# Gates of tokens 32 to 127 for the upper 64 expert blocks: from one-hot matmuls to indirect transfers

## The reference, cut to what matters

```
q = (xc @ wq).reshape(PEER_CHUNK, PEER_HEADS, 2, PEER_QDIM // 2)
sc = einsum('thpd,pkd->thpk', q, subkeys)
sv, si = top_k(sc, 16)
cv, ci = top_k((sv[:, :, 0, :, None] + sv[:, :, 1, None, :]) flattened, 16)
i1, i2 = the two key numbers of each chosen pair
e = i1 * 128 + i2                       # one of 16384 experts
g = softmax(cv)
act = gelu(einsum('td,thkd->thk', xc, u[e]))
out = einsum('thk,thkd->td', g * act, v[e])
```

## Time and profile before

| what | value |
|---|---|
| median of 3 runs | 1022.46 us (1022.28 to 1023.46) |
| the profiled execution | 1022.54 us, of it 1020.7 us span from the first to the last instruction |
| PE busy | 1011.5 us, 99% of the span |
| DVE, ACT, POOL busy | 834.3, 649.5, 459.3 us |
| granted clock of TensorE | 1.00 in every slice |
| first half of U, second half of U, V | about 270 to 457, 457 to 654, 654 to 1017 us |

### The profile page before, as it was taken

How to read it: one execution, slowest core, us unless ns; L and a number is a source line. 1 busy time by engine, 2 the same in 40 slices (tenths; PEclk the granted TensorE clock), 3 DMA queues, 4 the chain that set the end, 5 groups by cost and what they waited for, 6 DMA issues and landing times.

```text
span 1020.7 us, 20443 instructions
## 1 busy us (share of the span) xinstructions
PE 1011.5 (99%) x6302; PEld 894.7 (88%) x6302; DVE 834.3 (82%) x1611; ACT 649.5 (64%) x1192; POOL 459.3 (45%) x308
## 2 busy tenths in 40 slices
PE   8999999999999999999999999999999999999998
PEld 6798989999999999998888888888888888888887
DVE  6768786788899999988788888898888887777775
ACT  6456777666555444567877887877777764554543
POOL 0010321008148858867777770134344345545453
PEclk9999999999999999999999999999999999999999
DMA  8664565556467776666677775566665666666663
GB/s 328 264 216 151 187 198 179 187 168 223 146 166 191 190 190 167 184 180 176 173 177 165 174 176 170 162 223 192 205 197 196 206 232 225 211 219 221 211 224 115
DMA packets 89473, 198.20 MB, mean 194 GB/s; under 512 B 26320, under 2 KB 42832, under 8 KB 89424
## 3 DMA queue, kind: packets, MB, share of 16 engines
q1 hardware_dynamic: 68544, 188.99, 56.2%
q0 software_dynamic: 20736, 8.46, 7.3%
q10 hardware_dynamic: 144, 0.14, 0.1%
HBM read 187.01 MB, written 10.55 MB: 194 GB/s over the span
## 4 chain that ended last, share of the span: by engine, by line
PE 95%; DVE 3%; ACT 1%; DMA 1%; issue 0%; SPq 0%; POOL 0%; ACTq 0%; DVEq 0%
PE bank L900 34%; PE bank L875 12%; PE bank L876 6%; PE bank L831 5%; PE bank L833 5%; PE bank L832 5%; PE bank L385 2%; PE bank L844 2%; PE bank L386 2%; PE bank L387 2%; PE bank L451 2%; PE bank L771 2%; PE bank L455 1%; PE bank L467 1%; PE bank L468 1%; PE bank L469 1%
## 5 line engine op out<-in xcount | busy, mean ns | idle before, releaser
L1211 ACT ACTIVATE hi<-raw 128x1024 fp32r<-128x1024 f32 x253 | 269.0, 1063 | 260.7 <-PE bank L900 130.2
L1720 DVE TENSOR_TENSOR lo<-raw,hi 128x1024 fp32r<-128x1024 f32 x253 | 310.9, 1234 | 96.0 <-ACT hi L1211 92.3
L2036 POOL DMA_INDIRECT gate_d<-chosen_w,chosen_at x128 | 250.0, 1953 | 104.4 <-issue 50.5
L2053 POOL TENSOR_TENSOR auxl<-big,auxh 128x256 fp32r<-128x256 f32 x127 | 160.7, 1265 | 196.5 <-ACT auxh L1238 196.4
L875 PE MATMUL bank<-x,hi 128*128 128x512 f32 x512 | 183.9, 401 | 0.0
L900 PE MATMUL bank<-hi,auxh 128*128 128x512 f32 x504 | 157.2, 393 | 1.4 <-POOL auxl L2060 1.4
L900 PE MATMUL bank<-hi,auxl 128*128 128x512 f32 x504 | 155.7, 390 | 0.0
L900 PE MATMUL bank<-lo,auxh 128*128 128x512 f32 x504 | 155.5, 390 | 0.0
L831 PE MATMUL bank<-x,hi 128*128 128x256 f32 x512 | 145.3, 284 | 1.5 <-DVE lo L1720 1.5
L832 PE MATMUL bank<-x,hi 128*128 128x256 f32 x512 | 144.9, 283 | 0.0
L833 PE MATMUL bank<-x,lo 128*128 128x256 f32 x512 | 144.9, 283 | 0.0
(11 more groups left out here) (395 smaller groups left out, 1802.2 us busy)
## 6 DMA issues: line engine op xcount, KB each, us to landing
raw<-u_d SPq DMA_DIRECT2D x128, 512.0 KB
raw<-v_d SPq DMA_DIRECT2D x128, 512.0 KB
raw<-wpre_d SPq DMA_DIRECT2D x70, 512.0 KB
gate_d<-big POOLq DMA_DIRECT2D x16, 512.0 KB, 5.3
gring<-gate_d SPq DMA_DIRECT2D x128, 64.0 KB, 3.0
big<-wpre_d SPq DMA_DIRECT2D x8, 512.0 KB, 9.1
gate_d<-chosen_w,chosen_at POOLq DMA_INDIRECT x128
big<-x_d SPq DMA_DIRECT2D x4, 256.0 KB, 3.9
```

Source lines behind the costliest of these rows:

```text
L1211: act.activation(hi[:, slot(n), :], raw[:, splits(n) % RING, :], ACT.Copy).then_inc(hi_done, 1)
L1720: dve.tensor_tensor(lo[:, slot(n), :], raw[:, splits(n) % RING, :], hi[:, slot(n), :].bitcast(F32), ALU.subtract).then_inc(lo_done, 1)
L2036: pool.indirect_dma_start(gate_d, bass.IndirectOffsetOnAxis(chosen_at[:, d:d + 1], 0), chosen_w[:, P + d:P + d + 1], None, compute_op=ALU. ...
L2053: pool.tensor_tensor(auxl[:, s * T:(s + 1) * T], big[:, bass.ds(i * (UNROLL * T) + b * T, T)], auxh[:, s * T:(s + 1) * T].bitcast(F32), AL ...
```

## The change: what it does

1. Blocks 64 to 127, tokens 64 to 127: a second table `mid_d`. Each choice of a token has one of two cells, by whether its number is under 64 or not, so that one indirect transfer carries two choices of each of 64 tokens. 64 transfers.
2. Blocks 64 to 127, tokens 32 to 63: a third table `few_d`, with four cells, and four choices of each of 32 tokens in a transfer. 32 transfers.
3. The one-hot groups of blocks 64 to 127 are left for tokens 0 to 31: 8 groups in place of 32, one every eighth tile of V. V's first half is written out in place of a loop of 12 steps.
4. POOL issues these 96 transfers after its 128 old ones, and ahead of them 10 small transfers that move addresses and weights between partitions. SP waits for all of them before it loads tile 64 of V and what comes behind it. Both new tables are cleared by 8 transfers each (the upper half of each table), in the attention stage.
5. POOL no longer splits the gated blocks of V's first half: `w_lo` for blocks 0 to 63 is on DVE now. POOL takes it up again from block 64.
6. In V's second half SP fetches three pieces for a block, and DVE adds the two cells (`mid_sum`), sums the four (`few_sum`), and multiplies 224 columns in place of 128 (`gate_block_mid`).
7. DVE makes the addresses of the new transfers (8 small operations) at the end of U's first half.

```diff
+MID = P // 2
+FEW = P // 4
+NGRP_V = FEW // 4
...
-        gring = sb("gring", [P, GRING, P])
+        gring = sb("gring", [P, GRING, 3 * P])
...
             each_tile(sp, HALF - GRING, v_and_gates)
...
-            each_tile(sp, HALF, lambda i, j: v_and_gates(i, HALF - GRING + j))
+            sp.wait_ge(mid_scattered, 16 * MID)
+            sp.wait_ge(few_scattered, 16 * FEW)
+            each_tile(sp, HALF, lambda i, j: v_and_gates(i, HALF - GRING + j, mid=True))
...
             def g_and_v(i, j):
-                if j % 2 == 0:
-                    g_group(i, NGRP + 1 + j // 2, GT)
+                if j % 8 == 0 and j < 8 * (NGRP_V - 1):
+                    g_group(i, NGRP + 1 + j // 8, GT)
                 v_tile(i, j, 1)
...
+            def mid_sum(i, m):
+                dve.wait_ge(gate_in[m % GRING], ...)
+                parts = gring[:, m % GRING, P:2 * P]
+                dve.tensor_tensor(parts[:, MID:P], parts[:, 0:MID], parts[:, MID:P], ALU.add).then_inc(S("mid_summed"), 1)
...
+            def few_sum(i, m):
+                parts = gring[:, m % GRING, 0:P].rearrange("p (z t) -> p t z", z=4)
+                dve.tensor_reduce(gring[:, m % GRING, P + FEW:P + MID], parts, AXX, ALU.add).then_inc(S("few_summed"), 1)
...
             def v_step(i, j):
+                mid_sum(i, j + GRING)
                 loop_lo(i, V0 + j + SPLIT)
-                gate_block(i, j + GRING)
+                few_sum(i, j + GRING)
+                gate_block_mid(i, j + GRING)
...
+            def v_step_g(i, j):
+                g = NGRP + 1 + j // 8
+                w_lo(i, j + SPLIT - 1)
+                if j % 8 == 0 and j < 8 * (NGRP_V - 1):
                     add_parts(i, g, GT)
...
                 loop_lo(i, V0 + j + SPLIT)
                 gate_block(i, j + GRING)
...
@@ gpsimd
+                for z in range(2):
+                    clear(8 + 2 * p + z, mid_rows, "mid_cleared")
+                for z in range(2):
+                    clear(8 + 2 * p + z, few_rows, "few_cleared")
...
-            scatter(16 * NH - sent[0])
+            scatter(16 * NH - sent[0] - 16)
...
+            for z in range(4):
+                of_part = slice(z * FEW, (z + 1) * FEW)
+                pool.dma_start(few_at[of_part, :], mid_at[FEW:2 * FEW, of_part]).then_inc(S("few_moved"), 16)
+                pool.dma_start(few_w[of_part, :], chosen_w[FEW:2 * FEW, of_part]).then_inc(S("few_moved"), 16)
+            pool.wait_ge(S("few_moved"), 8 * 16)
+            pool.dma_start(mid_at[0:MID, MID:P], mid_at[MID:P, 0:MID]).then_inc(S("mid_moved"), 16)
+            pool.dma_start(chosen_w[0:MID, MID:P], chosen_w[MID:P, 0:MID]).then_inc(S("mid_moved"), 16)
+            scatter(16)
...
+            for d in range(MID):
+                if d and d % 16 == 0:
+                    pool.wait_ge(mid_scattered, 16 * d)
+                pool.indirect_dma_start(mid_d, bass.IndirectOffsetOnAxis(mid_at[:, MID + d:MID + d + 1], 0),
+                                        chosen_w[:, MID + d:MID + d + 1], None, compute_op=ALU.add).then_inc(mid_scattered, 16)
...
+            for d in range(FEW):
+                if d and d % 16 == 0:
+                    pool.wait_ge(few_scattered, 16 * d)
+                pool.indirect_dma_start(few_d, bass.IndirectOffsetOnAxis(few_at[:, d:d + 1], 0),
+                                        few_w[:, d:d + 1], None, compute_op=ALU.add).then_inc(few_scattered, 16)
...
-            w_lo_tokens(0, 0, "whi_tokens", 1, "wlo_tokens")
-            w_lo_tokens(0, 1, "whi_done", 1, "wlo_done")
-            each_tile(pool, NBLK - 1, lambda i, j: w_lo(i, j + 1))
+            pool.wait_ge(S("wlo_done"), HALF)
+            each_tile(pool, HALF, lambda i, j: w_lo(i, HALF + j))
```

More of the change, by code:

```diff
@@ L121, in build @@
         chosen_at = sb("chosen_at", [P, P], U32)
-        gring = sb("gring", [P, GRING, P])
+        mid_at = sb("mid_at", [P, P], U32)
+        few_at = sb("few_at", [P, FEW], U32)
+        gring = sb("gring", [P, GRING, 3 * P])
         gate_d = nc.dram_tensor("gate_d", (NBLK * P * P, 1), F32, kind="Internal").ap()
+        mid_d = nc.dram_tensor("mid_d", (NBLK * P * P, 1), F32, kind="Internal").ap()
+        mid_tiles = mid_d.rearrange("(e p t) o -> e p (t o)", e=NBLK, p=P)
+        mid_rows = mid_d.rearrange("(z p c) o -> z p (c o)", z=16, p=P)
+        few_d = nc.dram_tensor("few_d", (NBLK * P * P, 1), F32, kind="Internal").ap()
+        few_tiles = few_d.rearrange("(e p t) o -> e p (t o)", e=NBLK, p=P)
+        few_rows = few_d.rearrange("(z p c) o -> z p (c o)", z=16, p=P)
         gate_tiles = gate_d.rearrange("(e p t) o -> e p (t o)", e=NBLK, p=P)
@@ L243, in build @@
         scattered = sem("scattered")
+        mid_scattered = sem("mid_scattered")
+        few_scattered = sem("few_scattered")
         hi_done = sem("hi_done")
@@ L296, in each_tile, with each_tile_wide @@
                     body(0, j)
+        def each_tile_wide(eng, count, body):
+            for j in range(count):
+                body(0, j)
         block = ctx.enter_context(nc.Block())
@@ L1335, in v_step_g @@
             def v_step_g(i, j):
-                if j % 2 == 0:
-                    squares_b(i, NGRP + 2 + j // 2, GT)
+                if j % 8 == 0 and j < 8 * (NGRP_V - 2):
+                    squares_b(i, NGRP + 2 + j // 8, GT)
                 w_hi_gated(i, j + SPLIT - 1)
-                if j % 2:
-                    relu_b(i, NGRP + 2 + j // 2, GT)
+                if j % 8 == 2 and j < 8 * (NGRP_V - 2):
+                    relu_b(i, NGRP + 2 + j // 8, GT)
                 loop_hi(i, V0 + j + SPLIT)
@@ L1345, in v_step @@
                 loop_hi(i, V0 + HALF + j + 1)
-            each_tile(act, HALF - 4, v_step_g)
-            for m in range(HALF - 2, HALF):
+            each_tile_wide(act, HALF - 8, v_step_g)
+            for m in range(HALF - 6, HALF):
                 w_hi_gated(0, m)
                 loop_hi(0, V0 + m + 1)
-            act.wait_ge(S("weighed"), 1 + 2 * NGRP)
+            act.wait_ge(S("weighed"), 1 + NGRP + NGRP_V)
             each_tile(act, HALF - 1, v_step)
@@ L1830, in addresses, with mid_addresses, few_addresses @@
                                   ALU.mult, ALU.add).then_inc(S("chosen"), 1)
+            def mid_addresses():
+                late = slice(MID, P)
+                link(dve.scalar_tensor_tensor(caf[late, 0:P], i1f[late, 0:P], 128.0, i2f[late, 0:P], ALU.mult, ALU.add))
+                link(dve.tensor_scalar(caf[late, 0:MID], caf[late, 0:MID], -0.5, None, ALU.add))
+                dve.tensor_scalar(mid_at[late, :], caf[late, 0:P], float(P), tok_at[late, :],
+                                  ALU.mult, ALU.add).then_inc(S("chosen"), 1)
+            def few_addresses():
+                some = slice(FEW, 2 * FEW)
+                link(dve.scalar_tensor_tensor(caf[some, 0:P], i1f[some, 0:P], 128.0, i2f[some, 0:P], ALU.mult, ALU.add))
+                for z in (0, 2, 3):
+                    m = dve.tensor_scalar(caf[some, z * FEW:(z + 1) * FEW], caf[some, z * FEW:(z + 1) * FEW],
+                                          0.25 * (z - 1), None, ALU.add)
+                link(m)
+                dve.tensor_scalar(mid_at[some, :], caf[some, 0:P], float(P), tok_at[some, :],
+                                  ALU.mult, ALU.add).then_inc(S("chosen"), 1)
             spread(1)
@@ L1910, in _ @@
                 loop_lo(0, N_PRE + j + SPLIT)
+            mid_addresses()
+            few_addresses()
             dve.wait_ge(S("bank45_read"), NH + HALF // 2)
@@ L1937, in _, with w_lo, w_lo_tokens @@
             V0 = N_PRE + NBLK
+            def w_lo(i, b):
+                s = (V0 + b) % SPLIT
+                dve.wait_ge(S("whi_done"), i * UNROLL + (b + 1))
+                dve.tensor_tensor(auxl[:, s * T:(s + 1) * T], big[:, bass.ds(i * (UNROLL * T) + b * T, T)],
+                                  auxh[:, s * T:(s + 1) * T].bitcast(F32), ALU.subtract).then_inc(S("wlo_done"), 1)
+            def w_lo_tokens(b, tb, ready, count, done):
+                dve.wait_ge(S(ready), count)
+                c0 = (V0 + b) % SPLIT * T + tb * P
+                dve.tensor_tensor(auxl[:, c0:c0 + P], big[:, b * T + tb * P:b * T + (tb + 1) * P],
+                                  auxh[:, c0:c0 + P].bitcast(F32), ALU.subtract).then_inc(S(done), 1)
             def gate_block(i, m):
@@ L1948, in _ @@
             gate_block(0, 1)
+            w_lo_tokens(0, 1, "whi_done", 1, "wlo_done")
             gate_block(0, 2)
             gate_block(0, 3)
+            w_lo(0, 1)
             fold(0, HALF - 1)
@@ L1957, in v_step @@
             def v_step(i, j):
+                mid_sum(i, j + GRING)
                 loop_lo(i, V0 + j + SPLIT)
-                gate_block(i, j + GRING)
-            def v_step_g(i, j, keys=True, rows=True):
-                g = NGRP + 1 + j // 2
-                if j % 2 == 0:
+                few_sum(i, j + GRING)
[4 more added lines that the diff above has]
```

(22 more changed lines are left out.)

36 lines of the change are left out of this document (25 added, 11 removed).

## The result

The changed kernel takes 1052.71 us (median of 4 runs, 1048.62 to 1054.84) against 1022.38 before: a ratio of 1.0289, 95% interval 1.0251 to 1.0327. It is slower by 30 us. The forecast was 1059, range 1021 to 1072.

The account below looks back on a forecast made before the run. PE, busy 99% of the span, was taken to bound the kernel: 1022.5 less 11.8 for 24 groups, plus a 48.3 us stall of PE for the last transfer, gives 1059.0 us, range 1021 to 1072.

Parts of the forecast that it names:

- The gain: On PE in V's first half, 24 one-hot groups fewer at 0.49 us each save 11.8 us.
- what costs nothing: w_lo and second-half work on DVE, fetches, clears and address operations fit into idle time: together 0 to +6 us.
- The pace: In V's first half DVE's two-SBUF-input operations lock out POOL's transfers: one per tile, 2.72 us; chance 0.80.
- The start of the 80: First 16 of the 96 new transfers and a wait end at 655 us, where V begins; 80 are left.
- The number done by 823: 60 periods of 2.72 us from 655 to 822.5, two lost to waits and fetches: 58 transfers made, 22 left.
- The deadline: Tile 62 ends at 828.9; PE's tile 63 follows the last landing by 6.4 us; no stall means landing by 822.5.
- The sum: Last transfer starts by 869, lands by 870.8, PE goes on at 877.2: stall 48.3 us, total 1059.0 us.
- The ends: Range of the lock case: 1045 with four more transfers done and 5 us earlier, 1072 at the upper end.
- the upper case: Group tiles hold no transfer, each wait costs its period: nine more done late at 1.86, slower restart: 1072 us.

Follow-up runs that it names:

- e1: The changed kernel with its 32 four-part transfers left out, so tokens 32 to 63 get no gates in the upper blocks: 1010.58 us.
- e3: The changed kernel with w_lo of blocks 2 to 63 taken off DVE, ACT writing zeros in place of these low parts: 1052.51 us.
- e4: As e3, and loop_lo of V's tiles 3 to 62 writes only 512 of 1024 columns, the other low parts stale: 1020.14 us.
- e2: The changed kernel with the last 16 of its 32 four-part transfers left out: 1019.21 us.
- e5: A whole version of the changed kernel with only the 64 two-part transfers, 16 one-hot groups and no four-part table: 1015.08 us against 1022.13, ratio 0.9931.
- e6: The changed kernel with loop_lo and w_lo of tile 63 put ahead of the first mid_sum on DVE: 1053.07 us.

## Why the prediction was right, and where its sizes were off

- **The gain.** 24 x 0.49 = 11.8 us: shown by e1, which came out at 1010.58 where 1010.8 was worked out, with 11.2 of it inside V and 0.7 ahead of it. That also settles the part on what costs nothing: clears, addresses, `w_lo` on DVE, three fetches and three operations per tile in V's second half together cost no more than about half a microsecond net, as far as one run tells. DVE is still idle about 0.65 us per tile there (121.9 busy in the 160 from 880 to 1040); the three operations are 0.21, 0.38 and 0.41 long, more than the terms had.
- **The pace.** Between the groups it is one transfer per tile, 2.72 us, by a lock between a wait-free cost of 1.86 and the gaps of DVE's two-input operations: seen in the trace of after, and shown by e3 and e4 together. With 1.29 us of idle time per tile on DVE nothing changes, with 1.83 the free pace is there; where between them it turns was not measured. The rule of the exclusive lock in the Trainium skill (SBUF — State Buffer, Who interferes with whom) agrees with these rows; what it infers there, that a tensor_tensor doesn't stall a DMA from GpSimd, does not hold for these indirect ones (2.42 against 1.55 us beside tensor_tensor alone).
- **The start of the 80.** Given as 655; it was 652.5 for the first of them. The small transfers took 0.5 each, the first two 1.2, where I took 0.74; the wait behind them 2.9, as said.
- **The number done by 823.** 58 in the sum, 64 in the trace (from 652.5 to 822.3). This is the term that was mis-sized most: the sum let every tile hold one transfer, and only 38 of the 64 are of the long kind (2.35 us and more). The steps with a group shift DVE's rhythm, and two or three transfers of 1.55 to 1.9 slip in behind each. Five long idle times of POOL, 16 us in all, ate part of that. So 16 were left, not 22, and with the waits the last started at 856.0 where I had 869: 13 us.
- **The deadline.** Tile 62 ended at 829.0 (828.9 worked out). The sum let the last transfer land 1.8 us after its start, which is no more than its own time on POOL; SP woke 3.4 us after it, 1.6 more. From SP's waking to PE it was 7.4 us, not 6.4: PE waited not for `loop_lo` of tile 63 but for its `w_lo`, which stands behind `gate_block_mid` of block 64. The order of DVE showed that, and I had missed it.
- **The clock.** Not in the sum, since no row of before had PE at rest; it costs 1.8 us here, 2.9 in e2 and 2.1 in e4.
- **The sum.** The stall was 37.8 where 48.3 was forecast: 13 us less by the date, against it 1.6 by the landing and 1.0 by the restart. With the clock's 1.8 the forecast of 1059.0 becomes 1050.4, and the profiled execution took 1050.59. So the errors partly cancel, and the total came nearer than the stall did. Place, cause and sign were as forecast.
- **The ends.** Nine transfers more at 1.86 are 16.7 us, which puts the upper case at 1076 and not at the 1072 that is given; the lower one comes to about 1047, not 1045. Both the median and the profiled execution lie between 1047 and 1072, so nothing hangs on it.

## What to carry to other kernels

An engine with room in its busy share may still not have room for more work of a kind: ask at what pace this work goes beside the neighbour that it will stand beside, and whether the neighbour's gaps are about as long as one piece of it. If they are clearly shorter, the pace is the neighbour's period, and trimming the neighbour's work brings nothing (e3) until a gap is about as long as the piece (e4). And count up to a date: two thirds of this change's transfers were free and earned their matmuls (e5). The last sixth, 16 of the 96, started behind the date and cost over three times what all had earned, 39.6 us of stall and clock against 11.8.

## What the runs showed of the hardware that I had not expected

- A wait of TensorE of 4.3 us was enough to take the granted clock to 0.50, and the restart then ran at half pace for 6.1 us (e2). After rests of 7.0 (e4), 37.8 (after), 39.5 (e3) and 39.6 us (e6) it ran so for 4.3, 3.6, 4.3 and 6.1 us, so the length of the rest doesn't order it.
- An indirect transfer of 128 elements is held up only at its start: the one at 672.49 in after ends 1.5 us after it is let in, though `w_lo` runs meanwhile. A tensor_reduce that reads PSUM and a tensor_tensor with a PSUM input don't hold it up (e4: 1.55 us from 702.37 beside the one, 1.56 from 544.86 beside the other).
- The waits for the landing of sixteen indirect transfers and the gaps tied to nothing left POOL idle for 1.8 to 4.8 us each in V, and once for 6.3 (e6); in U, before, they were 2.7 to 3.1. This spread moves the date of the last transfer between runs, by 2.6 us from after to e6. That it is what sets after's runs 6 us apart is likely but not shown: only one of them is traced.
